# A two-layer encoder with routed experts: the last unit's rows added to the tokens by TensorE

## The chip, the core and the metric

One kernel, one launch, on one core of a Trainium2 chip. TensorE multiplies, VectorE and ScalarE work on tiles, GpSimd does the same from SBUF alone and issues the indirect transfers, SyncE issues most other transfers. The metric is the device time of the launch in microseconds (us), the median of several runs.

## The reference, cut to what matters

512 tokens of 1024 columns pass two layers. Each is a mixer, a layer norm, a mixture of experts and another layer norm. The part that the change touches:

```python
def _moe(h, router_w, w_gate, w_up, w_down):
    # each token picks one group of 4 experts and the top 2 of the 16 inside it
    ...
    def expert_block(args):
        xblk, e = args
        hid = jax.nn.silu(xblk @ w_gate[e]) * (xblk @ w_up[e])
        return hid @ w_down[e]
    ...
    y = jnp.zeros((T, D), h.dtype).at[buf_tok].add(yb * buf_gate[:, None].astype(yb.dtype))

for layer in range(DEPTH):
    y = mixer(h)                  # layer 0: retention and RG-LRU; layer 1: HGRN2, whose projection has v among its parts
    h = _layer_norm(DN_ALPHA * h + y, ln_w[layer, 0], ln_b[layer, 0])
    y = _moe(h, router_w, moe_w_gate[layer], moe_w_up[layer], moe_w_down[layer])
    h = _layer_norm(DN_ALPHA * h + y, ln_w[layer, 1], ln_b[layer, 1])
```

So every token gets two rows from the experts, each times its gate, and is then normalised. Everything is float32.

## The kernel before, in words

There is no scheduler: each engine has its own program, written out in order, and semaphores hold the engines together. An engine does its instructions in the order of its program.

*Expert stage.* The tokens lie in `h` as four tiles of 128 tokens (`NT = 4`) by 1024 columns. Each expert has 96 slots (`CAP`), so 16 experts fill 12 units of 128 slots (`NU = 12`), and a unit holds the rows of two experts. Tokens beyond 96 of an expert would go to extra units, at most ten (`MAXX`); their number `nx` is read from a table `tbl`, and every engine runs a loop `Fori(0, MAXX)` with `If(j < nx)` after its last unit. In this input `nx` is 0: ten turns are skipped. GpSimd scatters the token rows to their slots in HBM (`xs`, `slot_rows` in the trace); SyncE loads them unit by unit.

A unit on TensorE is: gate and up (`gate_up`), each 8 steps over the contraction, written as 32-row or 64-row strips because a unit has two experts; turning the next unit's rows (`turn_rows`); `down` of the unit before it; turning this unit's hidden rows (`turn_hidden`). On VectorE it is two multiplications (`hidden`, the second waits for up and makes `hid`), the copies of the turned rows (`copy_rows`) and of the turned hidden rows (`copy_hidden`). On ScalarE it is the sigmoid, and two copies of the result from PSUM to SBUF and a store to `xs` (`store`).

After the last store GpSimd gathers, for each tile t and each of the token's two experts k, the row of the slot `dst[:, t, k]` from HBM into `Yg` (8 indirect transfers of 128 rows). VectorE then handles tile by tile: two merges (`add_moe`: h = row * gate + h), statistics and standardising (`standardise`), scale and shift. In the second layer (n = 3) GpSimd does scale and shift of the first three tiles (`last_affine`). SyncE writes each tile to `out`.

*Between the two layers* TensorE waits for the weights `w_v1`, runs 24 matmuls with no use (`spin`), turns the first tile (`turn_h(2, 0)`) and then multiplies 64 times 512 columns for v. `w_v1` is loaded when down of unit 10 is done, to a place in `S` that an expert had.

## Time and profile before

| | |
|---|---|
| median of three runs | 1442.46 us (1441.6 to 1443.09) |
| the profiled execution | 1443.54 us, of it the span of the trace 1441.7 us |
| TensorE busy | 1353.0 us, 94% |
| VectorE busy | 509.8 us, 35% |
| ScalarE busy | 192.7 us, 13% |
| GpSimd busy | 196.7 us, 14% |
| mean granted TensorE clock | 0.971 of full speed |

A row of the chain or of a timeline begins with its start in us from the span's start and its length in us; "x16" is the number of instructions that it merges. In the rows a float32 matmul of 512 columns is two records. A bracket at the end of a row is how long the engine sat idle before it, and what released it; "issue" is time in which it waited for nothing that the profile shows. L577 is a line of the kernel before. L804 is ScalarE's copy helper and L424 the empty matmuls of `spin`.

### The profile page before, as it was taken

The page shows a single profiled execution, that of the slowest core. Times are in us where ns is not written, and L with a number is a line of the kernel's source. Part 1 is how long each engine was busy: PE and PEld are TensorE (multiplying, and loading weights), DVE is VectorE, ACT ScalarE, POOL GpSimd, SP SyncE. Part 2 cuts the span into 40 slices and gives each one's busy share as a digit, 9 for nine tenths or more (in the row PEclk, how much of TensorE's full clock was granted, in tenths as well). Part 3 has the DMA queues.
Part 4 walks back from the last instruction along what each step waited for, and adds up shares of the span by engine and source line. Part 5 has one row for each costly group of instructions (what it writes and reads, how often), then busy time and mean ns, then how long its engine had stood idle before and what let it go on. Part 6 is the DMA issues. An engine that isn't in the chain of part 4 may idle for free.

```text
span 1441.7 us, 16356 instructions
## 1 busy us (share of the span) xinstructions
PE 1353.0 (94%) x6807; PEld 629.5 (44%) x6807; DVE 509.8 (35%) x868; ACT 192.7 (13%) x325; POOL 196.7 (14%) x124
## 2 busy tenths in 40 slices
PE   8999999999999999799999999998899999999970
PEld 4444364663333333344555555554457433333320
DVE  1234854421111111440455656555355111111107
ACT  1125300100000000111111111121011000000010
POOL 0000400050000000200232323333102200000006
PEclk9999999999999999899999999999998999999995
DMA  9910244458999993753222201200266689999734
GB/s 350 354 61 1 107 185 204 175 204 309 408 415 422 414 423 123 273 130 117 59 59 59 59 10 49 58 0 0 91 288 261 228 340 428 405 427 408 312 144 154
DMA packets 83176, 306.80 MB, mean 213 GB/s; under 512 B 5476, under 2 KB 49832, under 8 KB 70696
## 3 DMA queue, kind: packets, MB, share of 16 engines
q1 hardware_dynamic: 61728, 262.81, 47.0%
q10 hardware_dynamic: 16776, 26.26, 5.0%
q0 software_dynamic: 4608, 16.78, 3.1%
q8 instruction: 52, 0.85, 0.2%
q14 instruction: 12, 0.10, 0.0%
HBM read 271.23 MB, written 34.60 MB: 212 GB/s over the span
## 4 chain that ended last, share of the span: by engine, by line
PE 67%; issue 19%; DVE 6%; POOL 3%; DMA 2%; ACT 1%; ACTq 1%; POOLq 0%; DVEq 0%
PE ps L549 23%; PE ps L577 11%; PE ps L452 8%; PE ps L509 7%; PE ps L661 4%; POOL W L1518 2%; PE ps L424 2%; PE ps L597 2%; PE ps L674 2%; PE ps L538 2%; DMA S<-w_in_odd 1%; PE ps L501 1%; DVE h L1226 1%; PE ps L490 1%; PE ps L565 1%
## 5 line engine op out<-in xcount | busy, mean ns | idle before, releaser
L549 PE MATMUL ps<-W,S 128*32 128x512 f32 (+1 forms) x2048 | 334.6, 593 | 2.0 <-DVE S L1326 2.0
L674 PE MATMUL ps<-hT,W 128*128 128x512 f32 x512 | 232.6, 593 | 0.7 <-ACT W L804 0.7
L549 PE MATMUL ps<-S 128*64 128x512 f32 (+1 forms) x512 | 222.9, 593 | 0.4 <-DVE S L1326 0.4
L577 PE MATMUL ps<-W,hT 128*32 128x512 f32 (+1 forms) x1024 | 169.8, 594 | 1.0 <-DVE hT L1340 1.0
L549 PEld LDWEIGHTS ps<-W,S 128*32 128x32 f32 (+1 forms) x2048 | 97.7, 113 | 146.1 <-issue 141.9
L674 PEld LDWEIGHTS ps<-hT,W 128*128 128x128 f32 x512 | 92.9, 191 | 90.3 <-issue 88.5
L577 PE MATMUL ps<-S,hT 128*32 128x512 f32 (+1 forms) x256 | 113.0, 594 | 1.0 <-DVE hT L1340 1.0
L1518 POOL TENSOR_TENSOR W<-S,sq 128x512 f32<-128x512 f32 x56 | 83.8, 1497 | 143.8 <-DVE S L1417 109.0
L804 ACT ACTIVATE hT<-ps 128x512 f32<-128x512 f32 x84 | 47.7, 599 | 380.6 <-PE ps L577 315.9
L549 PEld LDWEIGHTS ps<-S 128*64 128x64 f32 (+1 forms) x512 | 61.9, 123 | 71.6 <-issue 70.2
L1496 POOL DMA_INDIRECT W<-slot_rows,dst x16 | 16.0, 999 | 540.8 <-DMA slot_rows<-hT 536.6
L452 PE MATMUL ps<-W,hT 128*128 128x512 f32 x192 | 83.0, 593 | 0.7 <-ACT hT L804 0.7
L1417 DVE TENSOR_TENSOR S<-S 128x512 f32<-128x512 f32 x64 | 47.9, 748 | 93.5 <-PE ps L697 82.0
L697 PEld LDWEIGHTS ps<-S,W 128*128 128x128 f32 x448 | 57.7, 191 | 49.7 <-POOL W L1518 23.2
L577 PEld LDWEIGHTS ps<-W,hT 128*32 128x32 f32 (+1 forms) x1024 | 48.1, 113 | 69.5 <-issue 67.8
L697 PE MATMUL ps<-S,W 128*128 128x128 f32 x448 | 65.8, 291 | 12.8 <-POOL W L1518 12.8
L1331 DVE TENSOR_TENSOR hT<-hT,ps 128x512 f32<-128x512 f32 x24 | 16.5, 688 | 169.5 <-ACT hT L917 169.5
L1340 DVE COPY hT<-ps 128x512 f32<-128x512 f32 x24 | 16.6, 690 | 150.0 <-PE ps L565 150.0
L424 PE MATMUL ps<-sq 128*128 128x384 f32 x138 | 56.1, 569 | 12.8 <-DMA S<-w_in_odd 8.5
L1336 DVE TENSOR_TENSOR hT<-hT,ps 128x512 f32<-128x512 f32 x24 | 16.5, 687 | 134.6 <-PE ps L549 134.6
L509 PE MATMUL ps<-S 128*128 128x512 f32 x128 | 57.6, 594 | 1.0 <-DVE S L1369 1.0
L804 ACT ACTIVATE W<-ps 128x512 f32<-128x512 f32 x56 | 32.6, 597 | 180.3 <-PE ps L705 55.0
(209 smaller groups left out, 1404.3 us busy)
## 6 DMA issues: line engine op xcount, KB each, us to landing
W<-moe_w_gate SPq DMA_DIRECT2D x24, 2048.0 KB, 12.4
W<-moe_w_up SPq DMA_DIRECT2D x24, 2048.0 KB, 12.9
W<-moe_w_down SPq DMA_DIRECT2D x24, 2048.0 KB, 11.4
S<-moe_w_gate SPq DMA_DIRECT2D x8, 2048.0 KB, 12.9
S<-moe_w_up SPq DMA_DIRECT2D x8, 2048.0 KB, 14.0
S<-moe_w_down SPq DMA_DIRECT2D x8, 2048.0 KB, 16.9
W<-w_in_odd SPq DMA_DIRECT2D x32, 512.0 KB, 6.3
slot_rows<-hT ACTq DMA_DIRECT2D x24, 512.0 KB, 10.5
```

What stands on the lines that cost most here:

```text
L424: pe.matmul(ps[:, bank, 0:3 * P], ident, sq[:].rearrange("p a n -> p (a n)"), start=True, stop=True)
L452: last = pe.matmul(ps[:, 4 + n % 4, :], a, b, start=(c == 0), stop=(c == ND - 1))
L509: last = pe.matmul(ps[:, k, :], srcT[:, c, t * P:(t + 1) * P], w[:, c, half * 512:(half + 1) * 512], start=(start and c == tiles[0]), stop ...
L538: last = pe.transpose(ps[:, 4 + half, c * P:(c + 1) * P], xg[k][:, half * 4 + c:D:ND], ident)
L549: last = pe.matmul(ps[a:a + n, bank, :], xgT[:, c, a:a + n], w[L][slot_of(e)][:, c, :], start=(c == 0), stop=(c == ND - 1))
L577: last = pe.matmul(ps[a:a + n, 2 + half, :], hidT[:, c, a:a + n], wd[L][slot_of(e)][:, c, half * 512:(half + 1) * 512], start=(c == 0), st ...
L661: last = pe.matmul(ps[:, k, :], hT[:, c, t * P:(t + 1) * P], w_v1[:, c, (k % 2) * 512:(k % 2 + 1) * 512], start=(c == 0), stop=(c == ND - 1))
L674: last = pe.matmul(ps[:, f % 2, :], ring[slot][:, f, c, :], hT[:, c, :], start=(c == 0), stop=(c == ND - 1))
L697: last = pe.matmul(o, km[level % 2][:, c * P:(c + 1) * P], mixed(Q2, s, c * P, P), start=True, stop=True)
L804: return nc.scalar.activation(o, i, ACT.Copy)
L1417: v.tensor_tensor(k, k, view(src, at + step + 1, [[2, n], [-(step + 1), 2], [0, s]]), ALU.mult).then_inc(keys_updated, 1)
L1518: pool.tensor_tensor(view(km[level % 2], 0, [[2 * s, T // (2 * s)], [s, 2], [1, s]]), mixed(K2, s, 0, T), view(ones, 0, [[0, T // (2 * s)] ...
```

## The change

1. *The last unit's rows stay in SBUF.* ScalarE copies the result of unit 11 (`LAST`) to `y_last` and no longer stores it. VectorE builds in `last_gates` a matrix `last_sel` (tokens by the 128 slots of that unit) with the gate where a token owns a slot, and takes those gates out of `gts`, so that whatever is gathered for them counts nothing. TensorE turns the matrix once (in unit 3), VectorE copies it to `last_selT` (in unit 4). After the last down TensorE writes for each tile h + `last_selT` x `y_last` to PSUM: identity times h, 2 x 512 columns, then the matrix times `y_last`, 2 x 512 columns.
2. *The gathers wait for unit 10 only*, and `Yg` lies where nothing is in use any more. TensorE's order at the end is gate(11), down(10), up(11), turning, down(11).
3. *VectorE first does the merges of all four tiles*, then standardises tile by tile, reading the sums from PSUM. Standardising is three instructions of 1024 columns before (subtract and multiply, scale, shift) and two fused ones now; this is so in the mixers' norms too. GpSimd's `last_affine` is gone.
4. *Between the layers*: `w_v1` has another place and is loaded once up(11) is done, the `spin` is gone, `turn_h(2, 0)` stands ahead of the wait for `w_v1`, and the load of `masks` is behind the v projection.

```diff
@@ places
-        w_v1, w_out1 = S3(0, ND, D), S3(0, ND, D)
+        w_v1, w_out1 = W3(12288, ND, D), S3(0, ND, D)
...
-        Yg = W3(0, NT * 2, D)
+        Yg = [S3(0, NT * 2, D), W3(12288, NT * 2, D)]
+        y_last = xg[1]
@@ SyncE, expert stage
-                    elif L == 0 and u == NU - 1:
-                        sp.wait_ge(down_mm[0], 2 * (final_unit(NE - 3) + 1))
-                        sp.dma_start(w_v1, w_in_odd[0][:, D:2 * D].rearrange(rows, p=P)).then_inc(wout_in, 16)
                 sp.wait_ge(xgT_ps[L], NU * 2)
                 norm_scale(2 * L + 1)
                 norm_shift(2 * L + 1)
+                if L == 0:
+                    sp.wait_ge(up_mm[0], NU)
+                    sp.dma_start(w_v1, w_in_odd[0][:, D:2 * D].rearrange(rows, p=P)).then_inc(wout_in, 16)
@@ SyncE, between the layers
             head_weights(0, 0)
-            sp.dma_start(masks, c_masks).then_inc(masks_in, 16)
             head_weights(1, 1)
             sp.wait_ge(v_ps, 2 * NT)
+            sp.dma_start(masks, c_masks).then_inc(masks_in, 16)
@@ TensorE, expert stage
-                for u in range(NU):
-                    gate_up(u)
-                    if u + 1 < NU:
-                        turn_rows((u + 1) % 3, 16 * ((u + 1) // 3 + (1 if (u + 1) % 3 else 0)))
+                for u in range(LAST):
+                    gate(u)
+                    up(u)
+                    turn_rows((u + 1) % 3, 16 * ((u + 1) // 3 + (1 if (u + 1) % 3 else 0)))
                     if u > 0:
                         down(u - 1)
                     turn_hidden(u)
-                down(NU - 1)
+                    if u == 3:
+                        pe.wait_ge(last_built, L + 1)
+                        for t in range(NT):
+                            last = pe.transpose(ps[:, 7, t * P:(t + 1) * P], last_sel[:, t, :], ident)
+                        last.then_inc(last_turned, 1)
+                gate(LAST)
+                down(LAST - 1)
+                up(LAST)
                 pe.wait_ge(table_done, L + 1)
                 nx = pe.value_load(tbl[0:1, T_NX:T_NX + 1], min_val=0, max_val=MAXX)
+                copies = pe.value_load(tbl[0:1, T_COPIES:T_COPIES + 1], min_val=2 * NU, max_val=2 * (NU + MAXX))
+                turn_hidden(LAST)
+                down(LAST)
                 with pe.Fori(0, MAXX, 1) as j:
...
+                pe.wait_ge(last_copied, L + 1)
+                for t in range(NT):
+                    pe.wait_ge(merged, L * NT + t + 1)
+                    if t == 1:
+                        pe.wait_ge(y_copied[L], copies)
+                    for half in range(2):
+                        pe.matmul(ps[:, 2 * t + half, :], ident, h[:, t, half * 512:(half + 1) * 512],
+                                  start=True, stop=False)
+                    if t == 0:
+                        pe.wait_ge(y_copied[L], 2 * NU)
+                    for half in range(2):
+                        last = pe.matmul(ps[:, 2 * t + half, :], last_selT[:, t * P:(t + 1) * P],
+                                         y_last[:, half * 512:(half + 1) * 512], start=False, stop=True)
+                    last.then_inc(summed, 1)
@@ TensorE, between the layers
+            turn_h(2, 0)
             pe.wait_ge(wout_in, 32)
-            spin(7, 24)
-            turn_h(2, 0)
@@ ScalarE, expert stage
-                store(NU - 1, (NU - 1) % 2, 16 * ((NU - 1) // 2))
+                for half in range(2):
+                    act.wait_ge(down_mm[L], LAST * 2 + half + 1)
+                    copy(y_last[:, half * 512:(half + 1) * 512], ps[:, 2 + half, :]).then_inc(y_copied[L], 1)
@@ VectorE, standardise
-                done(v.reciprocal(col("rst1", t, 1), col("std", t, 1)))
-                ins = v.tensor_scalar(h[:, t, :], h[:, t, :], col("ag", 2 * t, 1), col("rst1", t, 1),
-                                      ALU.subtract, ALU.mult)
...
+                v.reciprocal(col("rst1", t, 1), col("std", t, 1))
+                if t == 0:
                     dve.wait_ge(lnp_in, 32 * (n + 1))
-                done(v.tensor_tensor(h[:, t, :], h[:, t, :], lnw, ALU.mult))
-                if n == 3:
-                    dve.wait_ge(ln_done, n * NT + t)
-                v.tensor_tensor(h[:, t, :], h[:, t, :], lnb, ALU.add).then_inc(ln_done, 1)
+                done(v.scalar_tensor_tensor(hh, src, col("ag", 2 * t, 1), lnw.rearrange("p (a n) -> p a n", a=2),
+                                            ALU.subtract, ALU.mult))
+                v.scalar_tensor_tensor(h[:, t, :], h[:, t, :], col("rst1", t, 1), lnb, ALU.mult, ALU.add
+                                       ).then_inc(ln_done, 1)
@@ VectorE, norm after the experts
+            def norm_moe(L):
+
+                for t in range(NT):
+                    dve.wait_ge(gathered[t], (L + 1) * 32)
+                    if t == 0:
+                        dve.wait_ge(h_scaled, L + 1)
+                    done(v.scalar_tensor_tensor(h[:, t, :], Yg[L][:, 2 * t, :], gts[:, t, 0:1], h[:, t, :],
+                                                ALU.mult, ALU.add))
+                    v.scalar_tensor_tensor(h[:, t, :], Yg[L][:, 2 * t + 1, :], gts[:, t, 1:2], h[:, t, :],
+                                           ALU.mult, ALU.add).then_inc(merged, 1)
+                for t in range(NT):
+                    dve.wait_ge(summed, L * NT + t + 1)
+                    standardise(2 * L + 1, t)
@@ VectorE, the matrix of gates, called in unit 1
+            def last_gates(L):
+
+                for k, slot in enumerate((r_t4, r_grk[:, 0:NT])):
+                    rel, inside = r_rel[:, k * NT:(k + 1) * NT], r_in[:, k * NT:(k + 1) * NT]
+                    done(v.tensor_scalar(rel, slot, -float(LAST * P), None, ALU.add))
...
+                    done(v.tensor_tensor(gts[:, :, k], gts[:, :, k], inside, ALU.subtract))
+                for t in range(NT):
+                    v.tensor_scalar(last_sel[:, t, :], iota[:, 0:P], r_rel[:, t:t + 1], r_in[:, t:t + 1],
+                                    ALU.is_equal, ALU.mult)
+                    done(v.tensor_scalar(last_tmp, iota[:, 0:P], r_rel[:, NT + t:NT + t + 1], r_in[:, NT + t:NT + t + 1],
+                                         ALU.is_equal, ALU.mult))
+                    ins = v.tensor_tensor(last_sel[:, t, :], last_sel[:, t, :], last_tmp, ALU.add)
...
@@ GpSimd
-                pool.wait_ge(y_stored[L][1], 16 * (NU // 2))
+                pool.wait_ge(y_stored[L][1], 16 * (LAST // 2))
                 pool.wait_ge(y_stored[L][0], stores)
...
-            last_affine()
```

The order on TensorE at the end of the first expert stage and behind it, before. L549 is gate and up (64 instructions of four strips: 32 for gate, 32 for up), L577 down, L565 the turning of hidden rows, L610 to L612 the read of the table and the loop (L588 belongs to a skipped turn), L424 the spin, L417 `turn_h`:

```order
L549 MATMUL ps<-W,S 32x512 x64
L577 MATMUL ps<-S,hT 64x512
L577 MATMUL ps<-W,hT 64x512
...
L565 MATMUL ps<-sq,hT 128x128 x4
L577 MATMUL ps<-W,hT 32x512 x32
L610 TENSOR_LOAD tbl
...
L612 COMPARE_AND_BRANCH
...
L611 COMPARE_AND_BRANCH
L424 MATMUL ps<-sq 128x384 x24
L417 MATMUL ps<-sq,h 128x128 x8
```

The same place now, where L554 is gate or up, L589 down, L577 the turning of hidden rows, L646 and L651 the sums of a tile, and L423 `turn_h`:

```order
L554 MATMUL ps<-W,S 32x512 x32
L589 MATMUL ps<-S,hT 64x512
L589 MATMUL ps<-W,hT 64x512
...
L554 MATMUL ps<-W,S 32x512 x32
L629 TENSOR_LOAD tbl
...
L577 MATMUL ps<-sq,hT 128x128 x4
L589 MATMUL ps<-W,hT 32x512 x32
...
L633 COMPARE_AND_BRANCH
L646 MATMUL ps<-h,sq 128x512 x2
L651 MATMUL ps<-S 128x512 x2
...
L423 MATMUL ps<-sq,h 128x128 x8
```

Down of unit 10 has moved between gate and up of unit 11, the reads of the table ahead of the turning, and four pairs of sums stand behind the loop where the spin was.

The order on VectorE behind the last unit of the first stage, before. L1336 makes `hid`, L1340 copies the turned hidden rows, L1352 to L1354 are the table and the loop, L1226 the merges, L1179 the statistics:

```order
L1336 TENSOR_TENSOR hT<-hT,ps 128x512 [waits hidT_in_psum_0,up_mm_0,act_mul_0]
L1340 COPY hT<-ps 128x512 [waits hidT_in_psum_0]
L1352 TENSOR_LOAD tbl [waits table_done]
...
L1354 COMPARE_AND_BRANCH
...
L1353 REGISTER_ALU
L1353 COMPARE_AND_BRANCH
L1226 SCALAR_TENSOR_TENSOR h<-W,gts,h 128x1024 [waits h_scaled,gathered_0]
L1226 SCALAR_TENSOR_TENSOR h<-W,gts,h 128x1024 [waits dve_order]
L1179 BN_STATS sm<-h 128x6 [waits dve_order]
```

The same place now, with the merges in L1245 and L1247 and the statistics in L1219:

```order
L1400 TENSOR_TENSOR hT<-hT,ps 128x512 [waits hidT_in_psum_0,up_mm_0,act_mul_0]
L1404 COPY hT<-ps 128x512 [waits hidT_in_psum_0]
L1420 TENSOR_LOAD tbl [waits table_done]
...
L1422 COMPARE_AND_BRANCH
...
L1421 REGISTER_ALU
L1421 COMPARE_AND_BRANCH
L1245 SCALAR_TENSOR_TENSOR h<-S,gts,h 128x1024 [waits h_scaled,gathered_0]
L1247 SCALAR_TENSOR_TENSOR h<-S,gts,h 128x1024 [waits dve_order]
...
L1245 SCALAR_TENSOR_TENSOR h<-S,gts,h 128x1024 [waits gathered_3]
L1247 SCALAR_TENSOR_TENSOR h<-S,gts,h 128x1024 [waits dve_order]
L1219 BN_STATS sm<-ps 128x6 [waits last_rows_summed]
```

All four tiles' merges stand ahead of the first statistics, and these wait for TensorE's sum.

## Rows read from the trace of the kernel before

**Rows 1.** The chain that ended last, second stage's end: start, length, what

```profile
1367.96 13.87 PE ps L549 x128
1381.83 7.02 PE ps L577 x32
1390.54 7.11 PE ps L577 x64
1398.30 2.67 DMA slot_rows<-hT
```

**Rows 2.** The same chain at the end of the first stage

```profile
566.03 7.04 PE ps L577 x32
573.09 17.14 DMA S<-w_in_odd
590.28 17.79 PE ps L424 x48
```

**Rows 3.** Timeline of TensorE, end of the first stage

```profile
574.71 7.07 PE L577 MATMUL ps<-W,hT 128*32 128x512 f32 x64 [0.98 <-DVE hT L1340]
...
607.90 1.04 PE L417 MATMUL ps<-sq,h 128*128 128x128 f32 x8
```

**Rows 4.** A stretch: length, busy times, granted clock, DMA share, GB/s

```profile
584.00:590.00 6.00, 0.00 (x0) 0.00 (x0) 0.00 (x0) 1.28 (x1) 0.00 (x0) 0.52 1.02 416
```

**Rows 5.** Timeline of VectorE, end of the second stage

```profile
1381.95 0.69 DVE L1336 TENSOR_TENSOR hT<-hT,ps 128x512 f32<-128x512 f32 x1 [5.61 <-PE ps L549]
1389.56 0.69 DVE L1340 COPY hT<-ps 128x512 f32<-128x512 f32 x1 [6.92 <-PE ps L565]
1407.96 2.60 DVE L1226 SCALAR_TENSOR_TENSOR h<-W,gts,h 128x1024 f32<-128x1024 f32 x2 [17.70 <-DMA W<-slot_rows,dst]
1410.60 1.29 DVE L1179 BATCH_NORM_STATS2 sm<-h 128x6 f32<-128x512 f32 x2
...
1412.78 0.81 DVE L1185 TENSOR_SCALAR h<-h,sm 128x1024 f32<-128x1024 f32 x1
...
1437.41 1.22 DVE L1196 TENSOR_TENSOR h<-h,S 128x1024 f32<-128x1024 f32 x1
```

**Rows 6.** Groups of VectorE by form: count, busy us, mean ns, idle before

```profile
L1211 DVE SCALAR_TENSOR_TENSOR h<-h,ps 128x512 f32<-128x512 f32 x8 | 5.5, 687 | 35.4 <-PE ps L509 35.4
L1299 DVE TENSOR_SCALAR S<-iota,S 128x128 f32<-128x128 f32 x8 | 1.7, 278 | 0.0
```

**Rows 7.** Timeline of VectorE, the first multiplication of a unit

```profile
1375.66 0.69 DVE L1331 TENSOR_TENSOR hT<-hT,ps 128x512 f32<-128x512 f32 x1 [6.97 <-ACT hT L917]
```

**Rows 8.** Timeline of GpSimd, the gathers of both stages

```profile
590.17 1.02 POOL L1496 DMA_INDIRECT W<-slot_rows,dst  x1 [270.64 <-DMA slot_rows<-hT]
...
1401.23 1.03 POOL L1496 DMA_INDIRECT W<-slot_rows,dst  x1 [265.91 <-DMA slot_rows<-hT]
...
1410.37 1.02 POOL L1496 DMA_INDIRECT W<-slot_rows,dst  x1 [0.30 <-issue]
```

**Rows 9.** Timeline of ScalarE, ends of both stages

```profile
582.47 0.34 ACTq L927 DMA_DIRECT2D slot_rows<-hT  x1
588.27 1.28 ACT L906 ACT_TABLE_LOAD   x1 [5.83 <-issue]
...
1398.30 0.34 ACTq L927 DMA_DIRECT2D slot_rows<-hT  x1
1403.60 1.28 ACT L906 ACT_TABLE_LOAD   x1 [5.33 <-issue]
```

**Rows 10.** Timeline of TensorE and VectorE at the mixers' last tile

```profile
273.34 1.09 PE L417 MATMUL ps<-sq,h 128*128 128x128 f32 x8 [0.45 <-DVE h L1196]
...
1085.72 0.81 DVE L1185 TENSOR_SCALAR h<-h,sm 128x1024 f32<-128x1024 f32 x1
1087.83 1.23 DVE L1196 TENSOR_TENSOR h<-h,S 128x1024 f32<-128x1024 f32 x1
1089.11 1.09 PE L417 MATMUL ps<-sq,h 128*128 128x128 f32 x8 [1.17 <-DVE h L1196]
```

**Rows 11.** Timeline of VectorE, first merge of the first stage

```profile
596.85 2.60 DVE L1226 SCALAR_TENSOR_TENSOR h<-W,gts,h 128x1024 f32<-128x1024 f32 x2 [22.39 <-DMA W<-slot_rows,dst]
```

More of the change, by code:

```diff
@@ L36 @@
 MAXX = 2 * T // (CAP + 1)
+LAST = NU - 1
 ALPHA = float((2.0 * DEPTH) ** 0.25)
@@ L186, in encoder_kernel @@
         r_blk = r_gt[:, 0:MAXX * NE]
-        T_NX, T_STORES = 10, 11
+        r_rel, r_in = (r_(2 * NT) for _ in range(2))
+        last_sel = rt[:, 0:T].rearrange("p (t n) -> p t n", t=NT)
+        last_selT, last_tmp = rt[:, T:2 * T], rt[:, 2 * T - P:2 * T]
+        T_NX, T_STORES, T_COPIES = 10, 11, 12
         diag = view(attn, 0, [[T + P, NT], [1, P]])
@@ L1362, in _ @@
             moe(0)
-            norm(1, add_moe(0))
+            norm_moe(0)
             def output(hd):
```

77 lines of the change are left out of this document (39 added, 38 removed).

## The prediction, made before the changed kernel ran

> **What bounds the kernel now.** I read the chain of work that ended last, since the share of busy time (TensorE 94%) is an average that says nothing of the two places where TensorE has stopped. In the second expert stage the chain lies on TensorE from unit to unit without a hole: gate and up of the last unit 1367.96 to 1381.83, down of the unit before it to 1388.85, down of the last 1390.54 to 1397.65. Then it leaves TensorE for the last store to HBM and the gathers, and nothing comes back [rows 1]. At the end of the first stage it goes to the load of `w_v1` (issued 573.09, 17.14 us) and to 48 records of the empty matmuls of `spin` [rows 2], though the last down has ended at 581.78 and `turn_h(2, 0)` starts at 607.90 [rows 3]. In that hole the granted clock is 0.52, about its lower level of 1.2 GHz [rows 4]. So there are two tails, 26.1 us of TensorE at rest or spinning and 44.0 us after its last matmul, and I forecast each by the engine that ends it last: TensorE in the first (what follows is its v projection), VectorE in the second.
>
> VectorE's second tail: first merge 1407.96, 2.64 us to the statistics at 1410.60, 2.18 us from there to the standardising at 1412.78; its last instruction ends at 1438.63, 3.1 us before the span does [rows 5].
>
> **The change, part by part.**
>
> *Order of the last unit.* down(10) now stands between gate(11) and up(11). down(10) thus ends half a gate-and-up earlier (13.87/2 = 6.94 us). But `hid` of the last unit has no down left to hide behind. Up to now VectorE began it 0.12 us after the last up (1381.95) for 0.69 us, and another 0.29 us goes from a VectorE end to a matmul (1390.25 to 1390.54): 1.10 us new on TensorE. The turning and copying behind it cost 1.69 us, as before (1388.85 to 1390.54) [rows 1, 5].
>
> *Transposes of `last_sel`.* Four of 128x128, like those of the hidden rows, which take 0.70 us (1388.85 to the copy at 1389.56): 0.70 us on TensorE in each stage, nothing covers it. With the 1.10 the last down ends 1.80 us later: 1399.45 in the second stage, 583.6 in the first.
>
> *`last_gates` on VectorE.* Twelve instructions of 128x128 at 0.28 us [rows 6] and ten on four columns, for which I take the same, come to 6.2 us, after the copy of unit 1, where VectorE idles 6.97 us every unit [rows 7]; even if they ran over, up of the next unit (6.94 us) hides it. The copy of the turned matrix (0.69 us) goes into the same hole: nothing. I put the additional 1x1 instruction of the table at nothing too; it would cost less than 0.28 us, and unit 0 runs meanwhile.
>
> *The gathers.* They wait for unit 10's store and no longer for unit 11's. From the end of a down to ScalarE's issue is 0.65 us (1397.65 to 1398.30), 2.93 us more to GpSimd's first gather at 1401.23, 6.73 us more until the first merge. The eight gathers start within 9.14 us, a pair every 2.6 us [rows 1, 5, 8], about what VectorE needs for a merge. Second stage: down(10) ends 1388.85 + 0.70 - 6.94 = 1382.61, issue 1383.26, first gather 1386.2, first pair there at 1392.9. First stage: 566.8, 567.5, 570.4, 577.1.
>
> *The loop over extra units.* This was hidden. Every engine runs `Fori(0, MAXX)` with ten skipped turns between its last unit and what follows. Now something stands behind it: VectorE's merges and TensorE's sums. ScalarE shows its length: from the end of its last DMA issue to the table load behind the loop are 5.46 us (582.81 to 588.27) and 4.96 us (1398.64 to 1403.60) [rows 9]. I take 5.2 us for VectorE and TensorE. From below it may be nothing (if the loop runs while the instruction ahead still waits); from above the trace of before only bounds it by VectorE's idle time, 17.70 us [rows 5] and 22.39 in the first stage [rows 11]. I take a middle: the branches are worked off while instructions ahead of them wait or run, but not ahead of an instruction with several waits, as `hid` is. VectorE's loop then starts when up(11) is done, at 1389.55 + 0.12 = 1389.67, and ends at 1394.9; TensorE's hides behind half a down (3.5 us) and shows 1.7 us.
> The Trainium skill, "Advanced Engine Details and Errata", Control Flow Timing, puts a compare-and-branch at about 108 ns; two of them in each of ten skipped turns would make 2.2 us, an estimate from that page, and with it the merges would be ready before the first pair of rows, so the sum would be that of the second rival. ScalarE's 5.0 to 5.5 us speak against so short a loop.
>
> *Second tail.* Merges from 1394.9, 4 x 2.64 = 10.6: 1405.4. TensorE's sums for tile 0 start at 1399.45 + 1.7 and take four matmuls of 512 columns at 13.87/16 = 0.87 us, so 1404.6, in time, and 3.5 us per tile is less than VectorE needs. Standardising a tile: 2.18 us, then two fused instructions at 1.32: 4.82, and 0.03 for reading PSUM (0.687 us for 512 columns from PSUM [rows 6] against 0.65 for half of one of 1024 [rows 5]): 4.85. Four: 19.4, end 1424.8 in place of 1438.63: **13.8 us off**. GpSimd's affine, which ran between the merges, is gone.
>
> *First tail.* TensorE's down ends 583.6, loop to 585.3, 16 matmuls of 0.87 us: 599.2, then `turn_h(2, 0)`, before at 607.90: **8.7 us off**. It needs tile 0 standardised: VectorE's merges from 573.9 + 5.2 = 579.1 end at 589.7, tile 0 at 594.5. Here the load of `w_v1` starts in the middle of the gathers (573.9). A pair is 1 MB; if both halve the rate the pairs come some 5 us apart, the last at 590, merges to 592.7, tile 0 at 597.6: still in time. `w_v1` itself, with its 17 us, is there at 591 to 594. The spin was there for the clock; TensorE now works until 0.7 us before the projection. ScalarE's next wait is the same. `masks` moves behind the projection on SP's queue, ahead of its first reader by three projections of a head (8 x 0.87 us each, 21 us), with `w_out1` behind it: nothing.
>
> *Mixer norms.* Three instructions (1085.72 to 1089.06, 3.34 us) become two at 1.32: 0.70 us. Only the last tile is on the chain: TensorE waited 1.17 us for it in the second mixer, 0.45 us in the first [rows 10], so **0.7 and 0.45 us off**.
>
> **Sum.** 13.8 + 8.7 + 0.7 + 0.45 = 23.6 us. The profiled execution was 1443.54 us (span 1441.7 and 1.8 around it), 1.1 over the median of 1442.46: from the median, **1419 us**.
>
> **Rivals.**
> 1. *The loops stand in full behind the last instruction.* VectorE's from 1392.05 (end of the hidden copy), merges from 1397.3: 11.4 us off. TensorE's from 583.6 to 588.8, turning at 602.7; in 5 us of rest the clock falls [rows 4], and the first matmuls run at the lower level, as those of the spin did (17.79 us for 24 of 384 columns, 0.65 us each at the speed above, so 2.2 lost): 3.0 us off. Total 15.5: 1427. For it: ScalarE's loop lay bare. Against: it stood behind a DMA issue with a wait on its own copies.
> 2. *The loops cost nothing.* Merges from the first pair, 1392.9: 15.8 us off; sums from 583.6: 10.4. Total 27.3: 1415. The trace does not exclude it, as both loops lay in idle time.
> The Trainium skill has a rule for it: "Perfetto Trace Analysis", DVE / Act Engine Instruction, lets an instruction wait for its semaphores in a queue while the sequencer goes on. No row of before shows that here.
> 3. *The gathers of the first stage are starved by the `w_v1` load.* If it takes its 17.1 us first and the last pair comes at 597, merges end 599.7, tile 0 at 604.5: 3.4 us off there, total 18.3: 1424. For it: before, beside that load, the store issued at 582.47 [rows 9] kept GpSimd until 590.17 [rows 8], 7.7 us in place of 2.9. Against: the first pair is issued, and mostly through, before it starts.
> 4. *Slower.* VectorE's loop is as long as its old idle time allows, 17.70 us in the second stage and 22.39 in the first [rows 5, 11], and stands behind the hidden copy. Then merges start at 1409.8 (end 1439.7, 1.1 us lost) and at 598.7 (tile 0 at 614.1, 6.2 lost): with the norms, 1448.6. It decides from 16.6 us a loop in the second stage; ScalarE's loop is a third of that.
>
> **How the numbers follow.** Forecast 0.45, rival 1 0.22, rival 2 0.18, rival 3 0.10, rival 4 0.03, others 0.02. The likeliest gives 1419 us. The range, 1413 to 1428, holds the forecast and rivals 1 to 3; its ends are rival 2 with 2 us for the gathers' first landing, and rival 1 with 1 us for unexpected waits. About 0.2% (3 us) is what a measurement of this kernel can tell from no change: faster 0.96, within 0.2% 0.02, slower 0.02.
>
> **What the profile of after would show.** VectorE's idle time before its first merge ending near 1393 (rival 2), 1395 (forecast) or 1397 (rival 1), and by "issue", not by the DMA; TensorE's gap between the last down and the sums, 0, 1.7 or 5 us, with the granted clock at 1.0 or about 0.5 in the sums; the four merges end to end; a tile standardised in 4.85 us; no hole before `turn_h(2, 0)`. The prediction is wrong if gathers of the first stage land after 595, if the merges or the reading of PSUM take longer beside the matmuls, or if one of the 0.7 us steps on TensorE pulls in a longer wait.

## The result, and the profile after

The changed kernel takes 1431.8 us (median of 4 runs, 1430.03 to 1432.64), the kernel before 1442.8 us beside it (1441.6 to 1443.31): ratio 0.9923, 95% interval 0.9906 to 0.9941. That is 11 us off, where 23.6 were forecast, and it lies outside my range of 1413 to 1428. The profiled execution took 1432.64 us, 1430.8 of it span.

I set the two traces side by side at the same instruction of TensorE, and wrote down how much earlier the changed kernel is there:

| where | before | after | earlier by |
|---|---|---|---|
| first mixer's norm, unit rows (128x128, x64) start | 293.26 | 291.45 | 1.8 |
| gate of the last unit, first stage | 552.16 | 550.75 | 1.4 |
| v projection starts | 609.68 | 607.92 | 1.8 |
| second mixer's norm, the same instruction | 1109.05 | 1106.86 | 2.2 |
| gate of the last unit, second stage | 1367.96 | 1366.21 | 1.8 |
| end of the span | 1441.7 | 1430.8 | 10.9 |

Counted from the gate of the last unit, the first tail gave 0.4 us (1.4 to 1.8) of 9.4 (8.7 and the 0.70 of the transposes, which lie ahead of this point), and the second 9.15 of 14.5 (13.8 and 0.70). The two executions differ a little ahead of the first change already: the turning of the first mixer's third tile starts at 266.84 in the kernel before and at 267.35 in the changed one, and this 0.5 us is in every row of the table. The timeline of TensorE at the end of the first stage shows where they stayed. L577 turns hidden rows, L589 is down, L646 and L651 the sums, L423 `turn_h`, L697 the v projection:

```profile
572.65 0.75 PE L577 MATMUL ps<-sq,hT 128*128 128x128 f32 x4 [0.87 <-DVE hT L1400]
574.38 9.51 PE L589 MATMUL ps<-W,hT 128*32 128x512 f32 x64 [0.98 <-DVE hT L1404]
589.36 3.75 PE L646 MATMUL ps<-h,sq 128*128 128x512 f32 x4 [5.47 <-issue]
592.90 3.01 PE L651 MATMUL ps<-S 128*128 128x512 f32 x4
595.75 1.88 PE L646 MATMUL ps<-h,sq 128*128 128x512 f32 x4
...
606.05 1.04 PE L423 MATMUL ps<-sq,h 128*128 128x128 f32 x8
607.92 4.53 PE L697 MATMUL ps<-W,hT 128*128 128x512 f32 x10 [0.83 <-ACT hT L840]
```

It answers to [rows 3]. Three things cost time against my plan. Down of the last unit takes 9.51 us in place of 7.07. Behind it TensorE waits 5.47 us by "issue", not by another engine, where I had 1.7. The sums of tile 0 then take 6.39 us (589.36 to 595.75), those of the others 3.43 each. The granted clock in these stretches lies between its two levels (1.2 and 2.4 GHz, 0.5 and 1.00 of full speed) and mostly near the lower one, in the second stage too. The windows show length, busy times of TensorE, its weight loads, VectorE, ScalarE and GpSimd, granted clock, DMA share and GB/s:

```profile
574.00:578.00 4.00, 3.62 (x20) 1.27 (x24) 0.12 (x1) 0.00 (x0) 3.09 (x4) 0.59 0.89 295
590.00:596.00 6.00, 6.00 (x9) 2.40 (x8) 2.57 (x2) 1.28 (x1) 0.00 (x0) 0.57 0.70 281
1391.00:1394.00 3.00, 3.00 (x20) 1.09 (x16) 0.00 (x0) 0.00 (x0) 2.39 (x3) 0.52 0.92 317
1404.00:1410.00 6.00, 6.00 (x10) 2.55 (x11) 4.16 (x5) 1.28 (x1) 0.00 (x0) 0.72 0.01 3
```

VectorE in the same tail (L1404 copies the turned hidden rows, L1245 and L1247 are the merges, L1219 the statistics; it answers to [rows 11]). The first merge comes 9.04 us after the copy, by "issue", and the third and fourth pair of rows are waited for:

```profile
573.43 0.69 DVE L1404 COPY hT<-ps 128x512 f32<-128x512 f32 x1 [0.84 <-PE ps L577]
583.17 1.28 DVE L1245 SCALAR_TENSOR_TENSOR h<-S,gts,h 128x1024 f32<-128x1024 f32 x1 [9.04 <-issue]
...
591.24 1.28 DVE L1245 SCALAR_TENSOR_TENSOR h<-S,gts,h 128x1024 f32<-128x1024 f32 x1 [2.95 <-DMA S<-slot_rows,dst]
...
596.59 1.28 DVE L1245 SCALAR_TENSOR_TENSOR h<-S,gts,h 128x1024 f32<-128x1024 f32 x1 [2.74 <-DMA S<-slot_rows,dst]
```

The second tail, VectorE and then TensorE, answers to [rows 5] and [rows 1]:

```profile
1389.38 0.69 DVE L1404 COPY hT<-ps 128x512 f32<-128x512 f32 x1 [0.84 <-PE ps L577]
1397.42 1.28 DVE L1245 SCALAR_TENSOR_TENSOR h<-W,gts,h 128x1024 f32<-128x1024 f32 x1 [7.35 <-issue]
...
1406.29 1.28 DVE L1247 SCALAR_TENSOR_TENSOR h<-W,gts,h 128x1024 f32<-128x1024 f32 x1
1409.38 1.30 DVE L1219 BATCH_NORM_STATS2 sm<-ps 128x6 f32<-128x512 f32 x2 [1.81 <-PE ps L651]
...
1426.47 1.28 DVE L1229 SCALAR_TENSOR_TENSOR h<-h,sm,S 128x1024 f32<-128x1024 f32 x1
```

```profile
1388.60 0.75 PE L577 MATMUL ps<-sq,hT 128*128 128x128 f32 x4 [1.36 <-DVE hT L1400]
...
1403.98 3.62 PE L646 MATMUL ps<-h,sq 128*128 128x512 f32 x4 [4.88 <-issue]
1407.39 1.96 PE L651 MATMUL ps<-S 128*128 128x512 f32 x4
1409.18 1.88 PE L646 MATMUL ps<-h,sq 128*128 128x512 f32 x4
```

The merges end at 1407.57, but the statistics wait another 1.81 us for TensorE's sum. So it is TensorE, not VectorE as I had it, that sets when the four tiles begin here; each tile then takes 4.57 us.

In the mixers' norms the wait of the last tile is gone in the first and 0.31 us in the second; these two rows answer to [rows 10]:

```profile
273.24 1.04 PE L423 MATMUL ps<-sq,h 128*128 128x128 f32 x8
...
1088.58 1.09 PE L423 MATMUL ps<-sq,h 128*128 128x128 f32 x8 [0.31 <-DVE h L1229]
```

### The profile page after: what moved, and what is told of

Its sections match the earlier page's. It is cut to its first block, busy times and chain, and to the rows that moved or that the text cites. A ratio compares the mean times of both kernels' runs of the same rounds, so it can differ in the third digit from the quotient of the medians.

```text
span 1430.8 us, 16437 instructions
## 1 busy us (share of the span) xinstructions
PE 1373.1 (96%) x6831; PEld 634.6 (44%) x6831; DVE 510.1 (36%) x906; ACT 192.7 (13%) x325; POOL 176.6 (12%) x118
## 4 chain that ended last, share of the span: by engine, by line
PE 68%; issue 20%; DVE 6%; POOL 3%; ACT 1%; ACTq 1%; DVEq 1%; POOLq 0%
PE ps L554 23%; PE ps L589 11%; PE ps L458 8%; PE ps L515 7%; PE ps L697 4%; POOL W L1577 2%; PE ps L609 2%; PE ps L710 2%; PE ps L544 2%; PE ps L430 1%; PE ps L507 1%; PE ps L577 1%; PE ps L496 1%; PE ps L483 1%; PE ps L646 1%
## 5 line engine op out<-in xcount | busy, mean ns | idle before, releaser
L554 PE MATMUL ps<-W,S 128*32 128x512 f32 (+1 forms) x2048 | 335.0, 593 | 2.0 <-DVE S L1390 2.0
L554 PE MATMUL ps<-S 128*64 128x512 f32 (+1 forms) x512 | 223.1, 593 | 0.4 <-DVE S L1390 0.4
L589 PE MATMUL ps<-W,hT 128*32 128x512 f32 (+1 forms) x1024 | 173.9, 607 | 1.0 <-DVE hT L1404 1.0
L554 PEld LDWEIGHTS ps<-W,S 128*32 128x32 f32 (+1 forms) x2048 | 97.5, 113 | 146.3 <-issue 142.3
L589 PE MATMUL ps<-S,hT 128*32 128x512 f32 (+1 forms) x256 | 114.7, 602 | 1.0 <-DVE hT L1404 1.0
L554 PEld LDWEIGHTS ps<-S 128*64 128x64 f32 (+1 forms) x512 | 61.8, 123 | 71.9 <-issue 70.5
L458 PE MATMUL ps<-W,hT 128*128 128x512 f32 x192 | 83.0, 593 | 0.7 <-ACT hT L840 0.7
L589 PEld LDWEIGHTS ps<-W,hT 128*32 128x32 f32 (+1 forms) x1024 | 49.3, 115 | 71.2 <-issue 69.5
L1404 DVE COPY hT<-ps 128x512 f32<-128x512 f32 x24 | 16.6, 691 | 137.9 <-PE ps L577 137.9
L458 PEld LDWEIGHTS ps<-W,hT 128*128 128x128 f32 x192 | 36.3, 190 | 46.3 <-issue 45.0
L515 PE MATMUL ps<-W,hT 128*128 128x512 f32 x128 | 55.7, 593 | 0.8 <-ACT hT L840 0.8
## 6 DMA issues: line engine op xcount, KB each, us to landing
S<-moe_w_up SPq DMA_DIRECT2D x8, 2048.0 KB, 13.8
slot_rows<-S ACTq DMA_DIRECT2D x4, 2816.0 KB, 19.4
```

The lines of the kernel that those rows point to most:

```text
L458: last = pe.matmul(ps[:, 4 + n % 4, :], a, b, start=(c == 0), stop=(c == ND - 1))
L515: last = pe.matmul(ps[:, k, :], srcT[:, c, t * P:(t + 1) * P], w[:, c, half * 512:(half + 1) * 512], start=(start and c == tiles[0]), stop ...
L554: last = pe.matmul(ps[a:a + n, bank, :], xgT[:, c, a:a + n], w[L][slot_of(e)][:, c, :], start=(c == 0), stop=(c == ND - 1))
L589: last = pe.matmul(ps[a:a + n, 2 + half, :], hidT[:, c, a:a + n], wd[L][slot_of(e)][:, c, half * 512:(half + 1) * 512], start=(c == 0), st ...
```

## The experiments

Two theories at the start. **A:** the ten skipped turns of the loop over extra units, some 0.8 us each, stand ahead of the merges and the sums; the rest (slow sums) follows from TensorE's rest behind them. **B:** the loops matter little; something with a fixed price, the read of the table or the gathers, holds the tails back. The expectations of the later runs state theories of their own under these letters. Each kernel ran beside the kernel before: 1442.5 us for the first four, 1443.1 for the next four, 1442.7 for the last two.

**e1_guard_all.** All four loops stand in a condition, so that they are jumped over whole when there are no extra units:

```diff
-                with pe.Fori(0, MAXX, 1) as j:
-                    with pe.If(j < nx):
+                with pe.If(nx > 0):
+                    with pe.Fori(0, MAXX, 1) as j:
+                        with pe.If(j < nx):
# the same on SyncE, ScalarE and VectorE
```

> The changed kernel with the loop over extra units put behind one branch (if nx > 0) on all four engines, so ten skipped turns become one skipped block. Theory A (the loops stand bare in front of the merges and the sums): VectorE's idle time before its first merge falls from 7.4 us to 3.5 us or less in the second stage (first pair of rows there at about 1391, so 2 us or less) and from 9.0 us to 3 us or less in the first; TensorE's gap before the sums falls from 4.9 and 5.5 us to under 1 us, the sums run at full clock (3.5 us a tile), and the median falls by 7 to 10 us, to 1422 to 1425. Theory B (the idle time is the table's read, the gathers or fetching, whatever the number of turns): both gaps stay above 4 us and the median within 2 us of 1431.8.

Measured: 1422.9 us (1422.47 to 1423.13), ratio to before 0.9865, 0.9848 to 0.9881, so 8.9 us less than the changed kernel. The gap by "issue" is gone on both engines. VectorE's merges in the first stage are now bound by the gathers (L1248 is the first merge of a tile here):

```profile
576.30 1.29 DVE L1248 SCALAR_TENSOR_TENSOR h<-S,gts,h 128x1024 f32<-128x1024 f32 x1 [2.50 <-DMA S<-slot_rows,dst]
...
583.09 1.28 DVE L1248 SCALAR_TENSOR_TENSOR h<-S,gts,h 128x1024 f32<-128x1024 f32 x1 [4.18 <-DMA S<-slot_rows,dst]
...
589.82 1.28 DVE L1248 SCALAR_TENSOR_TENSOR h<-S,gts,h 128x1024 f32<-128x1024 f32 x1 [4.13 <-DMA S<-slot_rows,dst]
...
595.17 1.28 DVE L1248 SCALAR_TENSOR_TENSOR h<-S,gts,h 128x1024 f32<-128x1024 f32 x1 [2.75 <-DMA S<-slot_rows,dst]
```

The pairs come 5.4 to 6.8 us apart. The v projection starts at 604.34, 3.6 us earlier than in the changed kernel (3.2 when counted from the gate of the last unit); the larger part, 6.4 us, is in the second tail, where sums start at 1395.53 without a gap.

**e2_five_turns.** The loops of TensorE and VectorE have 5 turns and not 10 (with no extra units the result is the same):

```diff
-                with pe.Fori(0, MAXX, 1) as j:
+                with pe.Fori(0, 5, 1) as j:
...
-                with dve.Fori(0, MAXX, 1) as j:
+                with dve.Fori(0, 5, 1) as j:
```

> The changed kernel with five turns instead of ten on VectorE and TensorE (it leaves out the last five possible extra units, of which this input has none). Theory A, each turn has a price: VectorE's gap falls by five turns at 0.6 to 0.9 us, from 7.4 to 3.0 to 4.4 us in the second stage; TensorE's by as much, to about 1 to 2 us, and the median falls by 4 to 7 us. If TensorE's sequencer runs ahead of half a down (3.5 us), its whole loop is about 9 us and five turns leave 1 us or less; if it does not, ten turns are 5 us and five leave 2.5. Theory B (a fixed price): the gaps stay.

Measured: 1422.0 us (1421.04 to 1422.78), ratio 0.9857, 0.984 to 0.9873. The gaps, of VectorE in the second stage and of TensorE in both:

```profile
1388.53 1.31 DVE L1245 SCALAR_TENSOR_TENSOR h<-W,gts,h 128x1024 f32<-128x1024 f32 x1 [3.00 <-issue]
```

```profile
584.92 1.95 PE L646 MATMUL ps<-h,sq 128*128 128x512 f32 x4 [1.54 <-issue]
...
1395.69 1.96 PE L646 MATMUL ps<-h,sq 128*128 128x512 f32 x4 [1.14 <-issue]
```

VectorE's gap fell from 7.35 to 3.00 us, which is 0.87 us a turn; TensorE's from 5.47 to 1.54 and from 4.88 to 1.14, 0.79 and 0.75 us a turn. Ten turns are thus 8.7 us on VectorE and 7.5 to 7.9 on TensorE, if all turns cost the same. VectorE's price is from the second stage alone. In the first its gap by "issue" is longer than ten such turns, 9.04 us in the changed kernel and 9.24 in e4 (8.24 in e10, without the load of `w_v1` beside it); what makes it longer is open. The sums of tile 0 run at full speed (1.79 us for the first four records, by the start of the next) once the rest ahead of them is short. By the median five turns are as good as none. In the traces the first tail is as short as in e1, since VectorE waits for the gathers there, and the second is 1 us longer.

**e3_guard_dve** and **e4_guard_pe.** The condition of e1 on VectorE alone, and on TensorE alone.

> The branch in front of the loop on VectorE alone. Theory A with TensorE as the one that ends the second tail (its sum of tile 0 ends at 1409.4, VectorE's merges at 1407.6): the merges start 4 us earlier but the statistics of tile 0 still wait for TensorE, the second tail gains under 0.5 us; in the first stage the last pair of rows (596.6) and TensorE's sums bound it, gain under 0.5 us. Median within 1.5 us of 1431.8. Rival (VectorE's merges are what ends both tails): 3 to 6 us faster.

> The branch in front of the loop on TensorE alone. Theory A: sums of tile 0 start right behind the last down (about 1399.5) and the clock stays up; then VectorE's merges (end 1407.6) are the bound of the second tail: 1.8 us gained there, and in the first stage the sums of tile 3 wait for the last pair of rows (596.6 + 2.6 = 599.2) and end 602.7 in place of 606.0: 3.4 us. Together about 5 us: median 1427. Rival (TensorE's loop costs nothing since VectorE bounds): within 1.5 us of 1431.8.

Measured: 1430.8 us (1429.27 to 1431.53; ratio 0.9916, 0.99 to 0.9933) and 1426.3 us (1426.04 to 1427.66; 0.9888, 0.9871 to 0.9904). In e3 VectorE's first merge in the second stage comes 0.91 us after the copy and not 7.35, and the statistics wait for TensorE all the same:

```profile
1389.86 1.28 DVE L1245 SCALAR_TENSOR_TENSOR h<-W,gts,h 128x1024 f32<-128x1024 f32 x1 [0.91 <-DMA W<-slot_rows,dst]
...
1408.26 1.30 DVE L1219 BATCH_NORM_STATS2 sm<-ps 128x6 f32<-128x512 f32 x2 [6.11 <-PE ps L651]
```

In e4 TensorE waits for the merges instead, and VectorE's loop is in the open:

```profile
1394.34 1.28 DVE L1246 SCALAR_TENSOR_TENSOR h<-W,gts,h 128x1024 f32<-128x1024 f32 x1 [7.42 <-issue]
...
1404.41 1.29 DVE L1220 BATCH_NORM_STATS2 sm<-ps 128x6 f32<-128x512 f32 x2
```

Alone VectorE's loop is worth 1.0 us, which is within the scatter of the runs, and TensorE's 5.5, both together 8.9. TensorE's is the one in front: VectorE's is worth 3.3 us once TensorE's is gone.

The trace of e3 shows something else in the first stage. The last down took 9.2 us although the granted clock was 1.00 all the way, behind the same two waits of 0.87 and 0.98 us as in the changed kernel; its last matmuls began late, behind nothing that the profile names:

```profile
575.26 5.35 PE L589 MATMUL ps<-W,hT 128*32 128x512 f32 x47 [0.98 <-issue]
581.07 3.41 PE L589 MATMUL ps<-W,hT 128*32 128x512 f32 x17 [0.46 <-issue]
```

```profile
575.00:584.50 9.50, 8.49 (x64) 2.55 (x64) 2.58 (x3) 0.60 (x1) 4.57 (x5) 1.00 1.01 408
```

**e5_norms_alone.** The kernel before, with the two fused instructions in the mixers' norms only:

```diff
+                if n % 2 == 0:
+                    v.reciprocal(col("rst1", t, 1), col("std", t, 1))
+                    if t == 0:
+                        dve.wait_ge(lnp_in, 32 * (n + 1))
+                    done(v.scalar_tensor_tensor(h[:, t, :], h[:, t, :], col("ag", 2 * t, 1), lnw,
+                                                ALU.subtract, ALU.mult))
+                    v.scalar_tensor_tensor(h[:, t, :], h[:, t, :], col("rst1", t, 1), lnb, ALU.mult, ALU.add
+                                           ).then_inc(ln_done, 1)
+                    return
```

> The kernel before with only the fused standardising of the two mixers' norms (two instructions for three). Theory A (a shorter wait of TensorE also keeps its clock up): the wait for the last tile falls from 0.45 to nothing and from 1.17 to 0.3-0.5 us, the logits and the spin behind it run at the upper level, and the unit loops start 1.85 us earlier in the first layer and 2.5 us earlier in the second, relative to their own mixer: 4.4 us in all, median about 1438. Theory B (the prediction's 0.70 us an instruction less and nothing else): 1.15 us, median about 1441.3. It also shows whether the granted clock in the last head of the second mixer (1.00 in the kernel before, 0.8 to 0.96 in every run with the change) stays at 1.00 when only the norms are changed.

Measured: 1439.9 us (median of 11, 1437.85 to 1441.21), ratio 0.9978, 0.9969 to 0.9987: 3.2 us off, for which the prediction had 1.15. In the profile the unit rows of the first mixer start at 290.24 (before 293.26), but 0.7 us of that is there already at the turning of the third tile (266.15 and 266.84), and it is no gain of the norms, since e9, which lacks them, has 265.95 there. From there the first mixer takes 24.1 us in place of 26.4, and the second 24.6 in place of 27.2 (third turning 1080.51 and 1081.89, unit rows 1105.15 and 1109.05): 2.3 and 2.5 us off. The granted clock of the 20 us in which the logits are made is 0.91, in the kernel before 0.83:

```profile
270.00:290.00 20.00, 18.48 (x85) 12.76 (x83) 12.80 (x54) 3.91 (x6) 1.16 (x2) 0.91 0.64 274
```

```profile
270.00:290.00 20.00, 19.55 (x83) 13.53 (x83) 11.46 (x41) 4.61 (x7) 0.00 (x0) 0.83 0.68 289
```

The first fence is e5, the second the kernel before. With a shorter wait the clock falls less, and the matmuls behind it (logits 3.67 us in place of 4.21, the spin behind them 6.75 in place of 7.88, from one start to the next) give the rest. These 4.9 us don't all reach the end, since the last head of the second mixer becomes slower (see "Given back elsewhere").

**e6_v_weights_late.** e1, and the load of `w_v1` waits until all eight gathers have landed:

```diff
                     sp.wait_ge(up_mm[0], NU)
+                    for t in range(NT):
+                        sp.wait_ge(gathered[t], 32)
                     sp.dma_start(w_v1, w_in_odd[0][:, D:2 * D].rearrange(rows, p=P)).then_inc(wout_in, 16)
```

> As e1 (the loops behind one branch), and the load of the v weights issued only when all gathers of the first stage have landed. Theory A (that load halves the rate of the gathers): the pairs come 2.6 us apart as in the second stage, the last at about 581 to 583 in place of 595.2, merges end by 587, the sums run through from 582.7 to 597, and the turning starts at about 597 in place of 602.4: 5 us off against e1, median about 1418. The v weights land at about 593, in time. Theory B (the gathers are slow by themselves, or the v weights become the bound): the turning or the first projection starts at 602 or later, median 1423 or more.

Measured: **1413.8 us** (1412.98 to 1414.7), ratio 0.9798, 0.9783 to 0.9813, the fastest version of all (with e7, within the scatter). The load is issued at 584.59 in place of 571.51, the pairs come 3.4, 2.8 and about 2.5 us apart (the load is issued when the last has landed), and the statistics follow the last merge at 587.05:

```profile
575.74 1.28 DVE L1250 SCALAR_TENSOR_TENSOR h<-S,gts,h 128x1024 f32<-128x1024 f32 x1 [2.83 <-DMA S<-slot_rows,dst]
...
579.18 1.28 DVE L1250 SCALAR_TENSOR_TENSOR h<-S,gts,h 128x1024 f32<-128x1024 f32 x1 [0.83 <-DMA S<-slot_rows,dst]
...
582.01 1.28 DVE L1250 SCALAR_TENSOR_TENSOR h<-S,gts,h 128x1024 f32<-128x1024 f32 x1 [0.23 <-DMA S<-slot_rows,dst]
...
584.54 1.28 DVE L1250 SCALAR_TENSOR_TENSOR h<-S,gts,h 128x1024 f32<-128x1024 f32 x1
585.85 1.28 DVE L1252 SCALAR_TENSOR_TENSOR h<-S,gts,h 128x1024 f32<-128x1024 f32 x1
587.05 1.29 DVE L1224 BATCH_NORM_STATS2 sm<-ps 128x6 f32<-128x512 f32 x2
```

The v projection starts at 597.57, 6.8 us before that of e1; 0.9 of that is there at the first mixer's unit rows already (290.23 and 291.10), so 5.9 us belong to the first tail. The span is 8.5 us shorter; 1.6 of it comes between the v projection and the second mixer's norm, where the granted clock at 1000 to 1015 is 1.00 in this profile and 0.89 in that of e1. That part belongs to the clock, not to the transfers. Without the gathers beside it the load takes 12.8 us and not 23.8, and so it lands at 597.4, just 0.2 us before the v projection: a later load would have held that back.

**e7_spin_in_waits.** e6, with one empty matmul (`spin(7, 1)`) ahead of the turning and one ahead of the last down, to shorten TensorE's rests (the empty matmuls change no result):

```diff
+                spin(7, 1)
                 turn_hidden(LAST)
+                spin(7, 1)
                 down(LAST)
```

> As e6, with one empty matmul of 384 columns ahead of the turning of the last hidden rows and one behind it, in the two waits of the last unit. Theory A (those two waits of 0.9 to 1.5 us and 1.0 us are what lowers the clock in the last down): down(11) takes 7.1 us in place of 8.8 in both stages and the granted clock there is 1.0; 1.5 us gained on TensorE per stage; the second stage is bound by TensorE's sums or VectorE's merges, so 1 to 3 us in all against e6, median about 1416. Theory B (the clock falls for another reason): down(11) still takes 8.5 us or more, and the median is e6's or up to 1 us above it.

Measured: 1414.5 us (1413.93 to 1415.46), ratio 0.9805, 0.979 to 0.982: no gain. The rests shrank (0.33 us ahead of the last down), and the clock did stay up: it is 1.00 through the last down, where e1 and e6 have about 0.81. That down still took 8.43 us (8.2 in the second stage):

```profile
575.13 8.43 PE L592 MATMUL ps<-W,hT 128*32 128x512 f32 x64 [0.33 <-DVE hT L1411]
```

```profile
575.00:583.50 8.50, 8.24 (x65) 2.43 (x65) 5.04 (x4) 0.60 (x1) 4.91 (x5) 1.00 0.93 346
```

So neither theory holds. Whether it was the empty matmuls that kept the clock up is shown for the second stage at most, where it is 1.00 in this profile alone of all with the new order; in the first, e3 has 1.00 without them. A slow last down has two parts. One is the clock: in e6, where nothing else is seen, it made 8.77 us of 7.07. The other comes at full clock, as in e3, 1.1 to 2.1 us in the profiles of e3 and e7. The gathers are under way in them, but so they are in e1 and e6. No run separates its cause.

**e8_old_order.** e1, with gate and up of the last unit together again, ahead of down(10):

```diff
                 gate(LAST)
-                down(LAST - 1)
                 up(LAST)
+                down(LAST - 1)
```

> As e1, but TensorE's old order at the end, gate and up of the last unit ahead of down of the unit before it, so that the wait for hid is covered and unit 10's store is 6.9 us later. If the reorder earns its place: pairs of rows come 6.9 us later in the second stage (first merge at about 1394.5, last merge end near 1406.5 in place of 1399.7), while TensorE is through 1.1 us plus about 1.7 us of clock earlier; the second tail is 5 to 7 us longer than in e1, and the first as much, since there too the last pair ends it: median 1432 to 1436. Rival (the wait for hid and the clock cost as much as the earlier store brings): within 2 us of e1's 1422.9.

Measured: 1430.6 us (1429.32 to 1432.16), ratio 0.9913, 0.9898 to 0.9928: 7.7 us slower than e1. The last down is at full speed again (573.26, 7.07 us), but the gathers start 10.3 us later in each stage (579.74 and 1391.26, e1 569.49 and 1380.90; counted from the gate of the last unit 10.0 and 7.0), the merges with them, and TensorE waits for VectorE:

```profile
589.08 3.75 PE L648 MATMUL ps<-h,sq 128*128 128x512 f32 x4 [8.75 <-DVE h L1250]
```

The order that I had costed at 1.10 us on TensorE (in truth 0.87 us in the first stage and 1.4 in the second, and 1.7 us of a slower down) pays well for itself. The same row shows the slow start of tile 0 (3.75 us) behind a rest that no loop made: it is the rest that counts. In the first stage the load of `w_v1`, issued at 564.65 here, is over before the gathers start, and the last pair is there as early as in e1 (595.1 and 595.2); the first tail is 3.1 us longer all the same, and the second 6.0.

**e9_before_guard.** The control: the kernel before, with the condition of e1.

> Control: the kernel before, with the loops over extra units jumped over whole when there are none. Theory A (the loops cost the changed kernel time because something stands behind them there, and cost the kernel before nothing, since they lay in idle time): the median within 1 us of before, 1442 to 1444; VectorE's idle time before its first merge still ends with the DMA. Rival (a skipped turn also keeps something in the kernel before, for instance ScalarE's table load or SyncE's queue): 2 us or more off, as a part of the 8.9 us that the same guard brought the changed kernel.

Measured: 1442.5 us (11 runs, 1440.72 to 1443.55), ratio 0.9998, 0.9989 to 1.0007. ScalarE gets to its table load 1.15 us after the store and not 5.33 ([rows 9] are its answers), and nothing comes of it, since VectorE's first merge waits for the DMA as in [rows 5]:

```profile
1398.66 1.28 ACT L908 ACT_TABLE_LOAD   x1 [1.15 <-issue]
```

```profile
1406.91 2.60 DVE L1229 SCALAR_TENSOR_TENSOR h<-W,gts,h 128x1024 f32<-128x1024 f32 x2 [17.38 <-DMA W<-slot_rows,dst]
```

So the loops cost the kernel before nothing that can be measured, and the changed one 8.9 us.

**e10_v_late_alone.** The changed kernel with its loops, and the delay of e6 alone.

> The changed kernel with its loops left in, and only the load of w_v1 held back until the eight gathers of the first stage have landed. Theory A (the gathers and the load slow each other down, and the last merge at about 599 is late for turn_h in the changed kernel too): the pairs land every 2.6 us, merges run from about 583 to 593.5, tile 0's sum at 596 bounds now, turn_h at about 602.5 in place of 606.05, 3 to 4 us off: about 1428. Rival (most of the 9.1 us between the guarded kernel with and without this delay came from the clock in the last head of the second mixer, not from the transfers): 0 to 1 us off, 1431 to 1432, with the merges where they were.

Measured: 1431.8 us (1430.57 to 1432.55), ratio 0.9926, 0.9912 to 0.9939, the same as the changed kernel. The merges follow one another from 581.92 to 592.07 as Theory A said, and yet nothing is won. Both stated theories missed the reason; the timeline of TensorE has it:

```profile
588.80 3.75 PE L648 MATMUL ps<-h,sq 128*128 128x512 f32 x4 [5.80 <-issue]
592.35 2.95 PE L653 MATMUL ps<-S 128*128 128x512 f32 x4
...
605.44 1.04 PE L425 MATMUL ps<-sq,h 128*128 128x128 f32 x8
```

From 588.80 to 605.44 TensorE adds the rows of four tiles without waiting for anyone. All four stand ahead of `turn_h`, so faster merges can't bring it forward. The same delay is worth 9.1 us by the medians once TensorE's loop is gone (in the traces 5.9 in the first tail and 1.6 of the clock), and nothing before.

## Why the prediction was wrong, by its own steps

**The failed step** is "I take 5.2 us for VectorE and TensorE", the length of the skipped loop, taken from ScalarE's row [rows 9]. It was marked as a middle with bounds; the mechanism was right, and the size was wrong in two ways. First, a skipped turn costs 0.87 us on VectorE and 0.75 to 0.79 on TensorE (e2), so ten make 8.7 and some 7.7 us: ScalarE's loop was no guide to the price on another engine. Second, I let TensorE hide 3.5 of 5.2 us behind half a down and see 1.7; it hid 2.4 to 2.6 us of 7.7 and showed 5.47 and 4.88. Those 2.4 to 2.6 are ten turns less the gap, counted back from the sums' start to before down's end.

From this step follows the next, "TensorE's sums for tile 0 ... 3.5 us". I had reckoned with a lower clock behind a rest only in rival 1; it came here: after 5 us of rest the first eight records of sums ran at a granted clock of 0.57 and took 6.39 us, in the second stage 5.2. And down of the last unit, put at 7.07, took 9.51 and 8.8, behind waits of 0.87 and 0.98 us (1.36 and 0.98 in the second stage) with a turning of 0.75 between them. In e8, with only the 0.98 us wait ahead, it took 7.07. The clock accounts for 1.7 us of it in each stage, by e6; the other 0.7 in the first stage is of the kind that e3 and e7 show at full clock, and its cause is open.

The first tail, predicted start of `turn_h` 599.2 less 0.45 of the first mixer, measured 606.05, 7.3 us late: the part ahead of down(11) came out 1.7 us earlier than planned, the slow down took 2.4 more, the gap 3.8, tile 0's sums 2.9, the other three 0.1 less. The second tail, 5.4 us short: the statistics of tile 0 began 6.4 us later after gate(11) than planned (2.1 until the end of down(11), 3.2 in the gap, 1.9 in tile 0's sums, against 0.8 that VectorE's later start had hidden in the plan), and the four tiles took 18.4 us and not 19.4.

**The rule cited with it.** The Trainium skill, "Advanced Engine Details and Errata", Control Flow Timing, gives about 108 ns for a compare-and-branch; two in each of ten turns would be 2.2 us, an estimate from that page. The runs disagree with that estimate: ten turns took 7.5 to 8.7 us, and 4.2 on ScalarE. It counts the two branches alone, and a turn has register instructions too; no run here times a single branch. The other, "Perfetto Trace Analysis", DVE / Act Engine Instruction, lets the sequencer go on while an instruction waits in a queue. The traces bear out little of it: in the second stage VectorE's loop, counted back by 8.7 us from the first merge, begins about when the multiplication that makes `hid` is done (1388.5); in the first stage it would begin only behind the copy (574.5). TensorE, of which that section does not speak, hid 2.4 to 2.6 us behind a running down.

**Rival 1** (loops in full, 1427) had the right place and price for the slow clock, and had ScalarE's 5.2 us too; with 8.7 and 7.7 us it would come to about 1433, close to the 1431.8 measured. Part of that would be luck, as it has neither the slow down nor the norms' extra gain. **Rival 2** (loops free, 1415) is what e1 makes of the kernel; it gave 1422.9, and 1413.8 once e6 took rival 3 out of it as well. **Rival 3** (gathers starved by the `w_v1` load) was right in its mechanism: the last pair at 596.6 in the changed kernel, where I had put it at 597. But it cost nothing there, as e10 shows, and 5.9 us in e1, as e6 shows. I had made it an alternative to the loops, and it lay in their shadow. **Rival 4** (slower) did not come; VectorE's loop was about half of its 16.6 us threshold.

**Right:** the mechanism and the amount of the fused norm in the last tail (4.57 us a tile, 4.85 forecast); the wait for `hid` (0.87 and 1.36 us, 1.10 forecast); the first gather in the second stage 18.1 us behind gate(11) (1384.35 less 1366.21; forecast 1386.2 less 0.7 of transposes less 1367.96, 17.5); `last_gates`, the copies and `masks` at nothing (no wait in the changed kernel names them). **Too dear:** the four transposes, 0.40 to 0.44 us a stage and not 0.70. **Too cheap:** the mixers' norms: 1.15 us forecast, 2.3 and 2.5 us at the norms themselves, in the changed kernel (24.1 and 24.6 us from the third turning) as in e5, and 3.2 net by the median of e5. I counted the wait that goes away and not the lower clock behind it.

**Given back elsewhere.** Between the v projection and the second mixer's norm the changed kernel needs 498.94 us and the kernel before 499.37, though the fused norm makes it 2.5 us less. In the changed kernel's last head of the second mixer the granted clock is lower with the same waits of 2.2 us:

```profile
998.00:1010.00 12.00, 9.18 (x32) 5.84 (x32) 5.45 (x8) 0.60 (x1) 3.86 (x3) 0.72 0.00 0
```

It is the same in e5, which has the norms and no other change; in e7 the clock stays at 1.00 there and the stretch takes 496.97 us, which is the 499.37 of before less the norm's 2.5. So 2.0 us are given back by the clock. Every profile with the fused norms but e7 has some of it, and both without have none. What decides it is open: I found no change in the program of that stretch, and these are single profiled executions.

## What to carry to other kernels

Before an instruction is put behind a loop that does nothing, price the loop on that engine, by a run with half the turns if no trace shows it: empty turns are free only as long as idle time covers them. When a change moves work into idle time, ask which engine next stands ahead of each consumer in program order, since a shadowed cost (here the contention of a load with the gathers) comes out only when the one in front is removed. Count a rest of TensorE twice, once for itself and once for the lower clock of the matmuls behind it, and look at the granted clock before the whole of a slow stretch is put down to it.

## What the runs showed of the hardware that I had not expected

- A skipped turn of `Fori` with `If` costs 0.87 us on VectorE, 0.75 to 0.79 on TensorE; on ScalarE ten turns took 4.2 us (5.33 less the 1.15 that are left with the condition). In the kernel before none of it shows.
- After two waits of 0.9 and 1.0 us with a 0.75 us turning between them, a down of 7.07 us at full speed took 8.8 to 9.5 in the changed kernel, its first part at a granted clock of 0.52 to 0.59. It is not the clock alone: where the clock stayed at 1.00, the down took 9.2 us (e3, first stage, the same waits) and 8.2 to 8.4 (e7, with empty matmuls in the waits). The cause of that second delay no run shows.
- Eight gathers of 128 rows, issued within 9 us, land a pair every 2.5 to 3.4 us beside TensorE's work (e6), and a pair every 5.4 to 6.8 us beside the load of `w_v1` (1024x1024 float32, 4 MB; e1). That load takes 23.8 us beside them and 12.8 behind them, so that issued 13 us later it lands 2 us later.
